# Depthwise taps of three of eight channel blocks moved to TensorE as diagonal matmuls, and VectorE's tap loop unrolled, in a two-block network kernel

## What is computed

```python
def conformer_conv(h, w_pw1, b_pw1, w_dw, b_dw, g_ln, b_ln, w_pw2, b_pw2):
    d = h.shape[-1]
    a = h @ w_pw1 + b_pw1
    a = a[..., :d] * jax.nn.sigmoid(a[..., d:])
    a = lax.conv_general_dilated(a, w_dw[:, None, :], window_strides=(1,),
                                 padding=[(CONV_WIDTH // 2, CONV_WIDTH // 2)],
                                 dimension_numbers=("NWC", "WIO", "NWC"),
                                 feature_group_count=d) + b_dw
    a = jax.nn.silu(layer_norm(a, g_ln, b_ln))
    return a @ w_pw2 + b_pw2
```

## Time and profile before

| what | us |
|---|---|
| three runs: median (lowest, highest) | 3458.18 (3446.76, 3460.39) |
| the profiled execution's own time | 3451.48 |
| its span in the profile | 3449.7 |
| TensorE busy, share of the span | 2860.3, 83% |
| VectorE busy | 1797.3, 52% |
| ScalarE busy | 946.8, 27% |
| taps L1935, 240 instructions, each | 0.472 |

### The profile page before, as it was taken

How to read it: one execution, slowest core, us unless ns; L and a number is a source line. 1 busy time by engine, 2 the same in 40 slices (tenths; PEclk the granted TensorE clock), 3 DMA queues, 4 the chain that set the end, 5 groups by cost and what they waited for, 6 DMA issues and landing times.

```text
span 3449.7 us, 37744 instructions
## 1 busy us (share of the span) xinstructions
PE 2860.3 (83%) x12514; PEld 1880.7 (55%) x12514; DVE 1797.3 (52%) x4182; ACT 946.8 (27%) x1987; POOL 1117.6 (32%) x1031
## 2 busy tenths in 40 slices
PE   7988877878777857787777778989779989897898
PEld 4424633333333626333333336987369989753798
DVE  0036376666664483666666644540535555315355
ACT  2145221211111102121221114430334444313344
POOL 0000177777777000777777771000000000000000
PEclk9989989999889978888998889999689999995999
DMA  7241699999999353999999994543025535330353
GB/s 235 85 166 41 246 403 387 396 396 392 381 375 397 102 191 124 380 371 388 389 383 397 367 389 176 182 141 130 23 86 182 182 130 182 123 129 0 123 182 134
DMA packets 223353, 818.11 MB, mean 237 GB/s; under 512 B 24832, under 2 KB 24960, under 8 KB 222336
## 3 DMA queue, kind: packets, MB, share of 16 engines
q0 software_dynamic: 147456, 536.94, 40.2%
q1 hardware_dynamic: 74160, 270.12, 23.1%
q10 hardware_dynamic: 1616, 9.55, 0.9%
HBM read 815.46 MB, written 1.05 MB: 237 GB/s over the span
## 4 chain that ended last, share of the span: by engine, by line
PE 55%; POOL 14%; DVE 13%; DMA 8%; issue 6%; ACT 3%; DVEq 0%; SPq 0%; ACTq 0%; POOLq 0%
PE ps L1168 12%; PE ps L1464 9%; PE ps L1424 7%; POOL arena L732 7%; POOL arena L740 6%; DMA arena<-experts_u,arena 6%; PE ps L1409 5%; PE ps L1410 5%; PE ps L1411 5%; PE ps L1174 3%; DVE arena L1875 2%; DMA weights<-stream 2%; PE ps L1571 2%; DVE arena L1935 1%; PE ps L1192 1%
## 5 line engine op out<-in xcount | busy, mean ns | idle before, releaser
L1464 PE MATMUL ps<-arena 128*128 128x512 f32 x2048 | 1017.9, 657 | 322.2 <-ACT arena L972 322.0
L1464 PEld LDWEIGHTS ps<-arena 128*128 128x128 f32 x2048 | 423.1, 211 | 909.3 <-issue 512.0
L1875 DVE SCALAR_TENSOR_TENSOR arena<-arena 128x1024 f32<-128x1024 f32 x512 | 620.6, 1226 | 477.8 <-DMA arena<-experts_u,arena 466.8
L732 POOL DMA_INDIRECT arena<-experts_u,arena x512 | 550.4, 1075 | 732.4 <-DVE arena L1859 573.8
L740 POOL DMA_INDIRECT arena<-experts_v,arena x512 | 554.3, 1083 | 156.1 <-issue 132.7
L1700 DVE TENSOR_TENSOR w_lo<-weights,w_hi 128x512 fp32r<-128x512 f32 x528 | 363.9, 691 | 293.9 <-ACT w_hi L823 293.8
L823 ACT ACTIVATE w_hi<-weights 128x512 fp32r<-128x512 f32 x528 | 332.0, 631 | 394.4 <-PE ps L1411 286.8
L1409 PE MATMUL ps<-a_hi,w_hi 128*128 128x256 f32 x1408 | 398.7, 283 | 5.2 <-DVE a_lo L1707 5.2
L1410 PE MATMUL ps<-a_lo,w_hi 128*128 128x256 f32 x1408 | 398.4, 283 | 0.0
L1411 PE MATMUL ps<-a_hi,w_lo 128*128 128x256 f32 x1408 | 398.4, 283 | 0.0
L1168 PE MATMUL ps<-sq,weights 128*128 128x256 f32 (+1 forms) x1472 | 334.0, 390 | 27.7 <-ACT sq L812 12.9
(11 more groups left out here) (212 smaller groups left out, 2790.6 us busy)
## 6 DMA issues: line engine op xcount, KB each, us to landing
weights<-stream SPq DMA_DIRECT2D x513, 512.0 KB, 3.3
arena<-experts_u,arena POOLq DMA_INDIRECT x512, 6.6
arena<-experts_v,arena POOLq DMA_INDIRECT x512, 6.7
arena<-rpb_windows ACTq DMA_DIRECT2D x4, 512.0 KB, 13.9
arena<-keys_in ACTq DMA_DIRECT2D x2, 1024.0 KB, 6.1
arena<-tab_mix ACTq DMA_DIRECT2D x2, 768.0 KB, 4.2
h_res<-x_cols ACTq DMA_DIRECT2D x1, 1024.0 KB, 5.3
arena<-ctx_cols ACTq DMA_DIRECT2D x1, 1024.0 KB, 11.3
```

The source lines that it names most:

```text
L732: pool.indirect_dma_start(out=u_ring[:, k % U_RING, :], out_offset=None, in_=experts_u[l], in_offset=bass.IndirectOffsetOnAxis(ap=expert[: ...
L1464: ins = pe.matmul(ps[:, 2 * b + half, :], diag[:, k % DIAGS, :], v_ring[:, k % V_RING, HALF * half:HALF * (half + 1)], start=(k == TOPK * ...
L1875: dve.scalar_tensor_tensor(out=u, in0=u, scalar=1.0, in1=h_rows[:, b, :], op0=ALU.mult, op1=ALU.mult, accum_out=act_raw[:, k:k + 1]).then_ ...
```

## The change

TensorE takes the taps of blocks 5, 6 and 7 (`TAPPED`): tap j of a block is a matmul with a diagonal 128x128 matrix of the channels' j-th weights as the stationary operand and the padded block, shifted by j, as the moving one; 31 of them accumulate in one PSUM bank, from which ScalarE copies them into `acc` with the bias. They stand behind `ada_blocks(3)`. The mean now waits for `conv_ready` and for `taps_copied`.

ScalarE builds the 93 diagonals: 16 in expert phase 0, one behind each of the groups 48 to 63, into the space of the sub-keys; eight ahead of the convolution's shift; and nine behind each sigmoid for the rest, into the rings of the experts' rows. VectorE keeps blocks 0 to 4, in code without loops: the first four gates, taps of blocks 0 and 1, the other four gates, taps of blocks 2, 3 and 4. ScalarE's loop over the sigmoids is unrolled too. The planner deals out three more banks.

```diff
--- before.py
+++ after.py
@@ -1,3 +1,4 @@
+import itertools
 import math
 from collections import namedtuple
 from contextlib import ExitStack
@@ -55,6 +56,8 @@
 CHOICES = TB * H
 CHOOSE_AT = {SPAN * i: i + TB for i in range(CHOICES - TB)}
 LEAD = 3
+TAPPED = [5, 6, 7]
+EARLY_TAPS = 16
 U_RING = 8
 V_RING = 12
 DIAGS = 8
@@ -300,6 +303,7 @@
     a["t_pw1"] = plan.tiles(8, 2)
     a["pw1"] = plan.products(4, 2, a["t_pw1"][1::2])
     ada(3, [1, 2, 3], 0)
+    a["taps"] = [plan.product() for _ in TAPPED]
     a["mean"] = plan.product()
     a["var"] = plan.product()
     a["t_pw2"] = plan.tiles(8)
@@ -467,8 +471,11 @@
         v_full = sq[:, 2 * T:4 * T].rearrange("p (b t) -> p b t", b=2)
 
         PAD = T + TAPS - 1
-        V = carve([("pad", KC * PAD), ("acc", KC * T), ("sg", 4 * T), ("tmp", 2 * T)])
+        V = carve([("diags", EARLY_TAPS * P), ("pad", KC * PAD), ("acc", KC * T), ("sg", 4 * T), ("tmp", 2 * T)])
         padded = V["pad"].rearrange("p (c t) -> p c t", c=KC)
+        tap_diags = [R[name][:, P * k:P * (k + 1)] for name, n in (("keys", EARLY_TAPS), ("u", U_RING * KC), ("v", 2 * KC))
+                     for k in range(n)]
+        assert len(tap_diags) >= TAPS * len(TAPPED)
         acc = V["acc"].rearrange("p (c t) -> p c t", c=KC)
         sig = V["sg"].rearrange("p (b t) -> p b t", b=4)
         pw_tmp = V["tmp"].rearrange("p (b t) -> p b t", b=2)
@@ -568,6 +575,9 @@
         w_ready = sem("w_ready")
         sig_ready = sem("sig_ready")
         conv_ready = sem("conv_ready")
+        tap_diag = sem("tap_diag")
+        gated_ready = sem("gated_ready")
+        taps_copied = sem("taps_copied")
         tap_done = sem("tap_done")
         centred = sem("centred")
         conv_act = sem("conv_act")
@@ -930,6 +940,11 @@
                     else:
                         copy_product(pr, oT[:, i, :], bank(pr)[:, 0:T])
 
+            def tap_diagonal(k):
+                c, j = TAPPED[k // TAPS], k % TAPS
+                act.activation(tap_diags[k], const("ident"), ACT.Copy, scale=col("w_dw", TAPS * c + j)) \
+                    .then_inc(tap_diag, 1)
+
             def peer(l):
                 pl = PL["peer", l]
                 key = f"peer{l}"
@@ -992,6 +1007,8 @@
                         gelu(n)
                     if n:
                         diagonals(n - 1)
+                    if l == 0 and GROUPS - EARLY_TAPS <= n < GROUPS:
+                        tap_diagonal(n - GROUPS + EARLY_TAPS)
                     if n in CHOOSE_AT:
                         gate_exps(CHOOSE_AT[n])
                     h = n // PER_HEAD + LEAD
@@ -1009,17 +1026,27 @@
                 pl = PL["conv"]
                 pre_norm(pl["norm"], "conv")
                 act.preload_act_table(ACT.Sigmoid)
+                for k in range(EARLY_TAPS, EARLY_TAPS + KC):
+                    tap_diagonal(k)
                 shift("conv", lambda c: a_in[:, c, :], lambda c: mod[:, 1, c, 0:1])
-                with act.Fori(0, 2) as i:
+                left = iter(range(EARLY_TAPS + KC, TAPS * len(TAPPED)))
+                for i in range(2):
                     for q, pr in enumerate(pl["pw1"]):
                         wait_product(act, pr, i)
 
                         act.wait_ge(bank_taken[pr.bank], i * pr.per + (pr.use - 1))
                         act.activation(sig[:, q, :], bank(pr)[:, T:2 * T], ACT.Sigmoid,
-                                       bias=cols[:, bass.ds(i * 4 + (COL["b_pw1"][0] + 8 + q), 1)]).then_inc(sig_ready, 1)
+                                       bias=col("b_pw1", 4 * i + 8 + q)).then_inc(sig_ready, 1)
+                        for k in itertools.islice(left, KC + 1):
+                            tap_diagonal(k)
                 for q in range(len(PL["ada", 3][1])):
                     ada_copy(3, q)
                 act.preload_act_table_set(ROOT_SET)
+                for c, pr in zip(TAPPED, pl["taps"]):
+                    wait_product(act, pr)
+                    taken(act.activation(acc[:, c, :], bank(pr)[:, 0:T], ACT.Identity, bias=col("b_dw", c)), pr)
+                wait_taken(act, pl["taps"][-1])
+                act.sem_inc(taps_copied, 1)
                 act.wait_ge(centred, 1)
                 act.activation(sq[:, :], V["acc"], ACT.Square).then_inc(centred, 1)
                 inverse_root(pl["var"], rstd[:, 0, :], D)
@@ -1506,7 +1533,16 @@
                                 .then_inc(tile_done[t.unit], 1)
                 claim(PL["ada", 3][2])
                 ada_blocks(3)
+                pe.wait_ge(gated_ready, KC)
+                for n, (c, pr) in enumerate(zip(TAPPED, pl["taps"])):
+                    claim(pr)
+                    for j in range(TAPS):
+                        pe.wait_ge(tap_diag, TAPS * n + j + 1)
+                        ins = pe.matmul(bank(pr)[:, 0:T], tap_diags[TAPS * n + j], padded[:, c, j:j + T],
+                                        start=(j == 0), stop=(j == TAPS - 1))
+                    finish(ins, pr)
                 pe.wait_ge(conv_ready, 1)
+                pe.wait_ge(taps_copied, 1)
                 sum_squares(pl["mean"], lambda k: acc[:, k, :], KC)
                 pe.wait_ge(centred, 2)
                 sum_squares(pl["var"], lambda k: sq[:, k * T:(k + 1) * T], KC)
@@ -1912,31 +1948,42 @@
                 dve.memset(padded[:, :, half + T:PAD], 0.0)
                 apply_norm("conv", pl["norm"], lambda c: h_res[:, c, :], lambda c: gain[:, 3, c:c + 1],
                            lambda c: a_in[:, c, :], scaled_ready)
-                with dve.Fori(0, 2) as i:
+
+                def gate(i):
                     for q, pr in enumerate(pl["pw1"]):
-                        dve.wait_ge(sig_ready, i * 4 + (q + 1))
-                        taken(dve.scalar_tensor_tensor(
-                            out=padded[:, bass.ds(i * 4 + q, 1), half:half + T].rearrange("p c t -> p (c t)"),
-                            in0=bank(pr)[:, 0:T], scalar=cols[:, bass.ds(i * 4 + (COL["b_pw1"][0] + q), 1)],
-                            in1=sig[:, q, :], op0=ALU.add, op1=ALU.mult), pr)
+                        c = 4 * i + q
+                        dve.wait_ge(sig_ready, c + 1)
+                        ins = dve.scalar_tensor_tensor(out=padded[:, c, half:half + T], in0=bank(pr)[:, 0:T],
+                                                       scalar=col("b_pw1", c), in1=sig[:, q, :], op0=ALU.add,
+                                                       op1=ALU.mult)
+                        taken(ins, pr)
                     wait_taken(dve, pl["pw1"][3], i)
-
-                    n = 0
+                    dve.sem_inc(gated_ready, 4)
+
+                done = [0]
+
+                def taps(chunks):
                     for j in range(TAPS):
-                        for q in range(4):
-                            a = acc[:, bass.ds(i * 4 + q, 1), :].rearrange("p c t -> p (c t)")
-                            x = padded[:, bass.ds(i * 4 + q, 1), j:j + T].rearrange("p c t -> p (c t)")
-                            w = cols[:, bass.ds(i * (4 * TAPS) + (COL["w_dw"][0] + TAPS * q + j), 1)]
+                        for k, c in enumerate(chunks):
+                            x = padded[:, c, j:j + T]
+                            w = col("w_dw", TAPS * c + j)
                             if j == 0:
-                                ins = dve.tensor_scalar(a, x, w, cols[:, bass.ds(i * 4 + (COL["b_dw"][0] + q), 1)],
-                                                        ALU.mult, ALU.add)
+                                ins = dve.tensor_scalar(acc[:, c, :], x, w, col("b_dw", c), ALU.mult, ALU.add)
                             else:
-                                dve.wait_ge(tap_done, i * (4 * TAPS) + (n - 3))
-                                ins = dve.scalar_tensor_tensor(out=a, in0=x, scalar=w, in1=a, op0=ALU.mult, op1=ALU.add)
+                                dve.wait_ge(tap_done, done[0] - len(chunks) + 1)
+                                ins = dve.scalar_tensor_tensor(out=acc[:, c, :], in0=x, scalar=w, in1=acc[:, c, :],
+                                                               op0=ALU.mult, op1=ALU.add)
                             ins.then_inc(tap_done, 1)
-                            n += 1
-                dve.wait_ge(tap_done, KC * TAPS)
+                            done[0] += 1
+
+                gate(0)
+                taps([0, 1])
+                gate(1)
+                taps([2, 3, 4])
+                assert done[0] == TAPS * (KC - len(TAPPED))
+                dve.wait_ge(tap_done, TAPS * (KC - len(TAPPED)))
                 dve.sem_inc(conv_ready, 1)
+                dve.wait_ge(taps_copied, 1)
                 pr = pl["mean"]
                 wait_product(dve, pr)
                 taken(dve.scalar_tensor_tensor(out=acc, in0=bank(pr)[:, 0:T].unsqueeze(1).to_broadcast([P, KC, T]),
```

## The result

The changed kernel takes 3466.03 us (median of 20 runs, 3444.84 to 3479.81), the kernel before 3450.39 (20 runs, 3437.96 to 3467.24): a ratio of **1.0042**, 95% interval 1.0027 to 1.0056. Of 3454 us that is +14.5, between +9.3 and +19.3. The change made the kernel a little slower, by less than the 0.5% that the prediction took as what can be told from no change. The profiled execution of the change took 3475.76 us, its span 3474.0.

The account below looks back on a forecast made before the run. The convolution's end was bound by VectorE, 27.2 us behind TensorE, which then becomes the bound. Mean start +15.5, mean -2.7, variance -0.7, diagonals +2.4 give +14.5 us on 3454.2, so 3468.7 us; range 3456 to 3487.

Parts of the forecast that it names:

- The bound moves to TensorE, in series with the run: End of the convolution: TensorE replaces VectorE as bound, 40.2 us of taps behind the modulation run against 27.2 us idle.
- VectorE: Five blocks of taps at 0.397 us a tap, ending near 1241, 13 us before TensorE reaches its taps.
- Taps, 40.2 us plus 1.9 for the waits: Behind the modulation run on TensorE: 93 matmuls at 0.432 us, plus 0.02 us for each wait on a diagonal.
- The estimate of 98 ns a pass: TensorE's taps: line between the skill's figures for 128 and 512 columns, giving 36.3 us; the prediction used the trace's 108 ns.
- Mean -2.7, variance -0.7: Norm behind the taps: TensorE just busy, so the mean is 2.7 us and the variance 0.7 us shorter.
- Eight diagonals before the shift, +2.4: ScalarE between table load and shift: eight uncovered diagonals delay TensorE's first product and all that follows by 2.4 us.
- The other 85 at nothing: ScalarE's 16 diagonals in the first expert phase and 69 behind the sigmoids are covered by waits: 0 us.
- The hand-over: Between taps and mean: ScalarE copies the third product (0.48 us) and hands back (0.1 us), a gap of 0.6 us.
- B: TensorE's taps: each wait empties the pipeline at 0.20 us, sum +31.2 us, 3485 us; chance 0.10.
- C: TensorE's taps run at the lower clock, 73.5 us, about +50 us, 3504 us; chance 0.05.
- D: TensorE's taps: products with a diagonal take one pass, 10 us for 93, sum -17.6 us, about 3437 us; chance 0.03.
- E: Later phases: turned bank rotation makes some claim wait less, the loss is made good, about 3454 to 3457 us; chance 0.09.

Follow-up runs that it names:

- t3: The change again, unaltered, with blocks 5, 6 and 7 on TensorE: 3470.26 us, ratio 1.0035 against the kernel before.
- diags_only: The change with its matmuls and ScalarE's three copies removed, all 93 diagonals kept, VectorE doing all eight blocks: 3457.49 us, ratio 1.0017 against the kernel before.
- no_before_shift: The change with the eight diagonals before the shift moved behind the sigmoids: 3624.44 us, ratio 1.0030 against the kernel before on a slower chip.
- one_wait: The change with one wait for all 93 diagonals ahead of the taps instead of 93: 3636.46 us, ratio 1.0059 against the kernel before on a slower chip.

## Why the prediction was right

It forecast +14.5 us and got +14.5 (+9.3 to +19.3) by the runs, 3468.7 against a median of 3466.03. The mechanism is right and shown. That the number fits to the digit is luck: the second measurement of the same kernel gives +12.1, the stages of the profiles give about +18, and the sum held a term of 1.9 us that doesn't exist and lacked the length of the modulation run. Point by point:

- **The bound moves to TensorE, in series with the run**: right, and shown by the series of 13.6 and 13.0 us a block and by 0.66 us between taps and mean in all of them. It was the term that decided: 40.2 us of new work against 27.2 us of idle time.
- **VectorE**: 0.397 us a tap in both rotations, done 17.7 us before the taps begin, where 13 was forecast; the difference is mostly the longer modulation run.
- **Taps, 40.2 us plus 1.9 for the waits**: the row of 42.10 matches the sum to the digit, and for a wrong reason. Waits cost nothing, by 40.41 with 93 and with one. The step that failed is "I take 0.02 us a wait". The 1.7 us were the clock in the row's first 3.45 us, 0.53, where the prediction said of the upper level that "the taps begin at it": as in the earlier trace rows, the clock was at 1.00 just ahead of the taps, and it fell all the same. In the second profile it stayed up, and the row was 40.41. The term should have been 40.4 with a clock risk of some 2 us. The estimate of 98 ns a pass worked out from the Trainium skill ("TensorE: Matmul & The Clock Gate", Back-to-back issue gap), which would have made the taps 36.3 us, doesn't hold for this stream: with four passes a matmul, 0.432 / 4 = 108 ns.
- **Mean -2.7, variance -0.7**: measured -2.63 and -0.68 in the first profile. In t3 the variance took 6.28 with the same gap ahead (and 5.10 to 6.64 in the others), so that -0.7 is not dependable; the mean's 3.69 came in every kernel with taps behind the run.
- **Eight diagonals before the shift, +2.4**: +2.3, in every profile. The other 85 at nothing: no cost of them is seen, though diags_only leaves room for a small one.
- **The hand-over**: 0.66 us for 0.6.
- **What it didn't foresee**: the modulation run 4.4 us longer in the first profile, which puts the stage at +18.3. The run of one kernel scatters by 2 us, and t3 has 52.9; part of it was this execution. The prediction treated the run's length as given, and gave it no share in the range.

Rivals B and C (a dear wait, the taps at the lower clock throughout) needed 5 us and 33 us more in the tap row; it has 0.2 to 1.9 over 40.2. D (one pass per diagonal) needed a row of 10 us. The Trainium skill ("TensorE: Matmul & The Clock Gate", Step-by-step) has 62 ns a MATMUL for decoding by microcode; nothing of it shows on top of the dense products' pace in these rows. E (made good later) isn't seen: the slowdown is in the runs. Of the two ways to count, the runs' interval reaches from 9.3 to 19.3 us, so whether the change costs more than 0.5% isn't excluded, only unlikely.

## What to carry to other kernels

Work moved off the engine that ends last in a stage gains at most the time by which it ends behind the next one, here 27 us, and the new work's full length counts against it when it stands behind that engine's own queue; compare the two numbers before choosing how much to move (one block gained here, two and three lost). If the receiving engine has gaps elsewhere, as TensorE had while it waited for weights, put the work into those gaps in program order: behind the run the taps began only after its last turn in every profile here, whatever gaps the run had. Where whole runs scatter more than the effect, read a stage between two landmarks inside a profile, and take a second profile before explaining a length of a transfer-bound stretch.

## What the runs showed of the hardware

- A satisfied semaphore wait ahead of a 128x256 float32 matmul costs nothing measurable: 186 records in 40.41 us with 93 waits (t3, no_before_shift) and with one (one_wait).
- Diagonal stationary operands are no cheaper: 0.432 us a matmul, the pace of the dense products.
- The granted clock can dip in a transfer-bound run that is only partly busy (0.85 over one run, 0.97 over others of nearly the same program). In two of seven profiles it also fell to the lower level as the dense row behind the run began (0.53 over its first 3.45 and 3.6 us, 1.00 just before), at 1.7 us each time.
- At the turn of a hardware loop with 128 vector operations in its body, VectorE stood for 4.46 us in one profile and 3.52 in another; the unrolled code has no such gap. Its cause isn't shown.
